# Residual adds, gate copies and normed tiles moved on VectorE's queue, and one weight tile on the queue of the DMAs, in a fused trunk layer

## What is computed

```python
def rms_norm(x, g):
    y = x * lax.rsqrt(jnp.mean(x * x, axis=-1, keepdims=True) + EPS)
    return y * g

def swiglu(x, wg, wu, wd):
    return (jax.nn.silu(x @ wg) * (x @ wu)) @ wd

def trunk_layer(x, ...):
    x = x + 0.5 * swiglu(rms_norm(x, g_ffn1), w_ffn1_gate, w_ffn1_up, w_ffn1_down)
    y, st = hybrid_mixer(rms_norm(x, g_mix), ..., w_in, b_gates, ..., w_out)
    x = x + y
    x = x + 0.5 * swiglu(rms_norm(x, g_ffn2), w_ffn2_gate, w_ffn2_up, w_ffn2_down)
    return x, st
# hybrid_mixer: p = rms_norm(x) @ w_in, cut into q, k, v, o (4 heads of an mLSTM),
# q, k, v, g (4 heads of a retention) and 8 gate rows; both scanned in chunks of 64
# tokens with carried states; the heads' normed outputs times w_out.
# At the end y = rms_norm(x, g_final), token by token, and the new states.
```

## Time and profile before

| | before |
|---|---|
| median of 3 runs | 1066.2 us (1065.99 to 1066.45) |
| profiled execution, its time | 1065.86 us |
| its span | 1064.1 us |
| TensorE, matmuls | 1040.7 us busy (98%), 8229 |
| TensorE, weight loads | 1030.3 us (97%), 8229 |
| VectorE | 792.1 us (74%), 1497 instructions |
| ScalarE | 515.3 us (48%), 943 |
| POOL | 215.1 us (20%), 190 |
| DMA | 142.14 MB, mean 134 GB/s |

### The profile page before, as it was taken

The page is one execution under the profiler, slowest core; times in us unless marked ns, Lnnn a source line. Parts: engine busy times, 40 slices in busy tenths (PEclk is TensorE's granted clock), DMA queues, the critical chain, the costliest instruction groups (busy, mean ns, idle before and its releaser), DMA issues.

```text
span 1064.1 us, 20973 instructions
## 1 busy us (share of the span) xinstructions
PE 1040.7 (98%) x8229; PEld 1030.3 (97%) x8229; DVE 792.1 (74%) x1497; ACT 515.3 (48%) x943; POOL 215.1 (20%) x190
## 2 busy tenths in 40 slices
PE   9999999999999979999999999999999999999996
PEld 8999999999999979999999999999999999999996
DVE  6985688987889866556655556588458889789986
ACT  6453366645665635333322223445336664466654
POOL 1100212222221211211332222210012222222120
PEclk9999999999999989999999999999999999999999
DMA  7536988789887566345354324543778888888852
GB/s 224 127 79 143 199 169 174 155 182 183 166 169 154 87 136 137 68 75 76 75 78 70 72 63 77 140 90 70 188 158 166 169 173 170 177 170 170 167 102 95
DMA packets 271963, 142.14 MB, mean 134 GB/s; under 512 B 10348, under 2 KB 269588, under 8 KB 271736
## 3 DMA queue, kind: packets, MB, share of 16 engines
q1 hardware_dynamic: 215736, 110.99, 42.2%
q0 software_dynamic: 56048, 29.79, 21.9%
q10 hardware_dynamic: 80, 0.02, 0.0%
HBM read 135.80 MB, written 3.29 MB: 131 GB/s over the span
## 4 chain that ended last, share of the span: by engine, by line
PE 82%; DVE 9%; issue 4%; DMA 2%; ACT 2%; SPq 0%; DVEq 0%; ACTq 0%
PE dense L857 35%; PE dense L733 34%; PE core_banks L857 4%; PE core_banks L733 3%; DVE w_lo L1732 3%; DVE h_raw L1762 1%; PE dense L803 1%; DMA w_raw<-in_w_in 1%; ACT w_hi L1269 1%; PE core_banks L1069 1%; PE core_banks L1084 1%; DVE h_op L1774 1%; DVE xT L1861 1%; PE core_banks L1087 1%; PE core_banks L1059 1%
## 5 line engine op out<-in xcount | busy, mean ns | idle before, releaser
L1269 ACT ACTIVATE w_hi<-w_src 128x512 fp32r<-128x512 f32 x182 | 113.2, 628 | 98.2 <-PE dense L857 55.8
L1269 ACT ACTIVATE w_hi<-w_raw 128x512 fp32r<-128x512 f32 x182 | 112.9, 629 | 82.7 <-PE dense L857 60.2
L857 PE MATMUL dense<-h_op,w_hi 128*128 128x272 f32 x768 | 147.9, 291 | 1.9 <-DVE xT L1861 1.7
L1732 DVE TENSOR_TENSOR w_lo<-w_raw,w_hi 128x512 fp32r<-128x512 f32 x182 | 123.8, 687 | 33.2 <-ACT w_hi L1269 31.6
L1732 DVE TENSOR_TENSOR w_lo<-w_src,w_hi 128x512 fp32r<-128x512 f32 x182 | 124.6, 688 | 29.8 <-ACT w_hi L1269 27.7
L733 PE MATMUL dense<-xg_hi,w_hi 128*128 128x272 f32 x672 | 142.3, 293 | 0.4 <-DVE rows L2197 0.4
L733 PE MATMUL dense<-xg_lo,w_hi 128*128 128x272 f32 x672 | 138.9, 288 | 0.0
L733 PE MATMUL dense<-xg_hi,w_lo 128*128 128x272 f32 x672 | 138.8, 287 | 0.0
L857 PE MATMUL dense<-x_late_hi,w_hi 128*128 128x272 f32 x432 | 125.8, 291 | 4.4 <-DVE rstd L1807 3.6
L857 PEld LDWEIGHTS dense<-h_op,w_hi 128*128 128x128 f32 x768 | 120.2, 188 | 4.6 <-DVE xT L1861 4.5
L857 PE MATMUL dense<-x_op_hi,w_lo 128*128 128x272 f32 x432 | 124.5, 288 | 0.0
(11 more groups left out here) (363 smaller groups left out, 2386.7 us busy)
## 6 DMA issues: line engine op xcount, KB each, us to landing
w_raw<-in_w_ffn_up SPq DMA_DIRECT2D x91, 256.0 KB, 4.2
w_src<-in_w_ffn_gate SPq DMA_DIRECT2D x90, 256.0 KB, 4.5
w_raw<-in_w_in SPq DMA_DIRECT2D x32, 512.0 KB, 9.2
w_src<-in_w_ffn_down SPq DMA_DIRECT2D x40, 256.0 KB, 4.3
w_raw<-in_w_ffn_down SPq DMA_DIRECT2D x40, 256.0 KB, 3.2
w_src<-in_w_ffn_gate POOLq DMA_DIRECT2D x36, 256.0 KB, 5.5
w_raw<-in_w_ffn_up POOLq DMA_DIRECT2D x36, 256.0 KB, 5.9
w_raw<-in_w_ffn_down SPq DMA_DIRECT2D x16, 384.0 KB, 6.1
```

Source lines behind the costliest of these rows:

```text
L857: last = nc.tensor.matmul(out, w[:, k, :], x, start=o in OPENS and k == 0 and m == 0, stop=k == KH - 1 and m == 2, skip_group_check=o not ...
L1269: nc.scalar.activation(block_of(w_hi, n, o), source(e, o), ACT.Copy).then_inc(block_hi, 1)
L1732: nc.vector.tensor_tensor(block_of(w_lo, n, o), source(g % 2, o), block_of(w_hi, n, o).bitcast(F32), ALU.subtract)\
```

## The change

Six moves; nothing is computed differently.

1. In a pair step, the h work (`sum_h`, `h_to_lo`) of a block product stands behind the copy out of the bank, where it stood ahead of it.
2. In an up step the two `split_lo` of `w_down` tiles stand one block product later (o = 4 and 6 in place of 3 and 5).
3. In the first down step of a chunk the adds to the residual stand further ahead, and the weight sum `sum_t2` behind the add of product 2.
4. At the mixer's start, the first w_in tile's rounding (ScalarE) and its low part (VectorE) stand behind the last two normed tiles and their squares; two of the sums of squares stand ahead of it, too.
5. SP issues the third w_in tile ahead of the last down step's blocks, in place of behind the first two tiles. Its wait for a slot is that of every plain tile.
6. At the end: the last pair's first two turns stand one block product later; one `last` turn goes into the last product ahead of its last tile of the sum; one chunk's scaling and one of VectorE's copies stand further ahead; in the last step of the second half two of the sums of squares stand two ranks earlier.

```diff
@@ load (SP) @@
-                if U_IN <= s < U_IN + RAW - 1:
-                    sp.wait_ge(block_lo, BLOCKS * STEP_LAST + (2, BLOCKS, 6, 6)[s % RAW])
+                if s in (U_IN, U_IN + 1, U_IN + 3):
+                    sp.wait_ge(block_lo, BLOCKS * STEP_LAST + (2, BLOCKS, 6)[s % RAW])
                 elif s >= RAW:
                     sp.wait_ge(w_lo_ready, s - RAW + 1 + step * i)
@@ ffn (SP) @@
                     for d in range(DOWNS):
+                        if step_of_down(n, c, d) == STEP_LAST:
+                            load_in(0, 2)
                         load_blocks(n, step_of_down(n, c, d), down_quarter(w_down, c, d))
...
+            def load_in(h, u):
+                col = (h // H) * 4 * H * P + u * H * P + (h % H) * P
+                load(0, U_IN + 4 * h + u, 0, w_rows(w_in)[:, :, col:col + P], DT)
...
-                    load(0, U_IN + 4 * h + u, 0, in_v[:, :, col:col + P], DT)
+                    if h or u != 2:
+                        load_in(h, u)
@@ down_pair (TensorE) @@
-                    turns = {1: 2 * d - 2, 2: 2 * d - 1} if d == DOWNS - 1 else {3: 2 * d - 2, 5: 2 * d - 1}
+                    turns = {2: 2 * d - 2, 3: 2 * d - 1} if d == DOWNS - 1 else {3: 2 * d - 2, 5: 2 * d - 1}
...
-                    part(o, range(KH)).then_inc(product_done, 1)
+                    if o == 6 and g == 2 * STEPS - 1:
+                        part(o, range(last_k))
+                        turn_last(1)
+                        part(o, range(last_k, KH)).then_inc(product_done, 1)
+                    else:
+                        part(o, range(KH)).then_inc(product_done, 1)
                 if g == 2 * STEPS - 1:
-                    turn_last(1)
                     turn_last(2)
@@ down_pair (ScalarE) @@
                     split_hi(0, U_GATE, 0)
-                    split_hi(0, U_IN, 0)
                     for j in (DT - 1, DT - 2):
                         x_ready(n, j)
                         normed_hi(0, j, None, G_MIX, 0)
                         square_end(n, j)
+                    split_hi(0, U_IN, 0)
@@ last_part (ScalarE) @@
                 scale_chunk(0, ACT_COLS)
+                scale_chunk(1, ACT_COLS)
                 last_times_gain(DT - 2, 1, 6)
-                scale_chunk(1, ACT_COLS)
@@ next_lo (VectorE) @@
-                elif g % STEPS == STEP_DOWN and o in (3, 5):
-                    split_lo(0, U_DOWN[n] + (o - 3) // 2, 0)
+                elif g % STEPS == STEP_DOWN and o in (4, 6):
+                    split_lo(0, U_DOWN[n] + (o - 4) // 2, 0)
@@ pair (VectorE): these lines go from ahead of the copies of o = 3, 4, 5 to behind them @@
                     if deferred:
                         for h_o in ((), (1,), (2,), (4, 5), (), (), ())[o] if e == 0 else ():
                             sum_h(n, k, h_o)
                         for h_o in (((), (), (), (), (0,), (1,), (3,)), ((2,), (4,), (5,), (6,), (), (), ()))[e][o]:
                             h_to_lo(n, k, h_o)
@@ down_pair (VectorE), d == 0 @@
                     h_to_lo(n, k, 3)
+                    take_down(n, c, d, 0)
                     h_to_lo(n, k, 2)
-                    take_down(n, c, d, 0)
+                    take_down(n, c, d, 1)
                     h_to_lo(n, k, 4)
-                    take_down(n, c, d, 1)
                     take_down(n, c, d, 3)
                     h_to_lo(n, k, 5)
                     next_lo(n, g - 1, 6)
-                    sum_t2(g + 1)
                     take_down(n, c, d, 2)
                     h_to_lo(n, k, 6)
+                    sum_t2(g + 1)
@@ down_pair (VectorE), d > 0 @@
+                    if g % STEPS == STEP_LAST and rank in ((1, 2) if n else (3, 4)):
+                        add_end(n, DT - 4 + (rank in (2, 4)))
...
-                    if g % STEPS == STEP_LAST and rank in (3, 4):
-                        add_end(n, DT - 4 + (rank == 4))
...
-                        if o == 5:
-                            split_lo(0, U_IN, 0)
-                            normed_lo(0, DT - 1, 1, G_MIX, 0)
-                            add_end(n, DT - 1)
...
                             scale_last(0, DVE_COLS)
+                            scale_last(1, DVE_COLS)
+                            take_last(1)
                 if g == STEP_LAST:
+                    normed_lo(0, DT - 1, 1, G_MIX, 0)
                     normed_lo(0, DT - 2, 1, G_MIX, 0)
+                    add_end(n, DT - 1)
                     add_end(n, DT - 2)
+                    split_lo(0, U_IN, 0)
                 if g == 2 * STEPS - 1:
...
-                    scale_last(1, DVE_COLS)
-                    take_last(1)
```

More of the change, by code:

```diff
@@ L671, in ffn @@
                     for d in range(DOWNS):
+                        if step_of_down(n, c, d) == STEP_LAST:
+                            load_in(0, 2)
                         load_blocks(n, step_of_down(n, c, d), down_quarter(w_down, c, d))
+            def load_in(h, u):
+                col = (h // H) * 4 * H * P + u * H * P + (h % H) * P
+                load(0, U_IN + 4 * h + u, 0, w_rows(w_in)[:, :, col:col + P], DT)
             ffn(0, w_ffn1_gate, w_ffn1_up, w_ffn1_down)
-            in_v = w_rows(w_in)
             for h in range(2 * H):
                 for u in range(4):
-                    col = (h // H) * 4 * H * P + u * H * P + (h % H) * P
-                    load(0, U_IN + 4 * h + u, 0, in_v[:, :, col:col + P], DT)
+                    if h or u != 2:
+                        load_in(h, u)
                 if h == 0:
@@ L1898, in pair @@
                         sum_t4(g + 1)
-                    if deferred:
-                        for h_o in ((), (1,), (2,), (4, 5), (), (), ())[o] if e == 0 else ():
-                            sum_h(n, k, h_o)
-                        for h_o in (((), (), (), (), (0,), (1,), (3,)), ((2,), (4,), (5,), (6,), (), (), ()))[e][o]:
-                            h_to_lo(n, k, h_o)
                     if o == 3:
@@ L1920, in pair @@
                             up_third_gated(p, Q)
+                    if deferred:
+                        for h_o in ((), (1,), (2,), (4, 5), (), (), ())[o] if e == 0 else ():
+                            sum_h(n, k, h_o)
+                        for h_o in (((), (), (), (), (0,), (1,), (3,)), ((2,), (4,), (5,), (6,), (), (), ()))[e][o]:
+                            h_to_lo(n, k, h_o)
                     if not (ends and o == 6):
```

## The result

The changed kernel took 1068.55 us (median of 9 runs, 1066.33 to 1070.79), the kernel before 1066.11 us (9 runs, 1065.86 to 1067.71) beside it: a ratio of 1.002, 95% interval 1.0011 to 1.0029. The forecast was 1059.2 us. The profiled execution of after is the slowest of its nine, 1070.79 us with a span of 1069.1 us, so the losses read from it are some 2 us larger in all than the median's.

The account below looks back on a forecast made before the run. TensorE's own work was taken to set the time, with some 13 us of waits to win in a 1064.1 us span. Gains 4.2 + 1.3 + 0 + 0.7 + 0.8 = 7.0 us gave 1059.2 us against the 1066.2 us median; range 1055.5 to 1063.8.

Parts of the forecast that it names:

- Pair steps: Gate steps' last block product: the copy out of the bank ends 0.35 us sooner, twelve times; 4.2 us gained (0 to 5.5).
- First down steps: First down step of each chunk: adds free the bank sooner; 0.33 us four times, 1.3 us gained.
- Second half step's down: Second FFN, w_down split behind up_second: the 0.8 us wait goes, but TensorE waits longer for the last SiLU; 0 gained (0 to 0.8).
- Mixer's order: Mixer's start: second w_in product 2.4 us sooner, less 1.7 us for the clock; 0.7 us gained (-1.0 to 2.4).
- The price of the clock: Mixer's start: 0 to 6.8 us at half clock behind 5.2 us of idle time costs half; middle taken, 1.7 us.
- (c): Rival, mixer's start: the clock holds through the moved idle time; 1057.5 us, chance 0.05.
- End: Kernel's end: a turn one product later, a square sum moved, less three turns in the last product; 0.8 us gained (-0.5 to 1.7).
- The third w_in tile: Last down step: issued early on SP, hidden by 5.8 us spare before VectorE reads the accumulated block; cost taken as 0.
- (d): Rival, last down step: early w_in tile holds up the blocks; slower, 1068.3 us if landing at 357.7; chance 0.12.
- the third of the prediction's signs of being wrong: Ahead of the last down step: the prediction is wrong if VectorE waits for a DMA there.
- (a): Rival, mixer: first two w_in tiles come sooner than 12.4 and 15.8 us, 6.8 us gained there; 1053.1 us, chance 0.08.
- (b): Rival, pair steps: they keep their wait since something other than gate_second ends it; 4.2 us missing, 1063.4 us, chance 0.12.

Follow-up runs that it names:

- e1: The kernel put back: the changed kernel, with SP issuing the third w_in tile behind the first two again, as before; 1058.3 us, ratio 0.9928.
- e10: The kernel before plus pair-step copies ahead of h work, w_down low parts one product later, and the new first-down-step order; 1059.52 us, ratio 0.994.
- e4: The kernel before with only the mixer's new order: last two normed tiles and their squares ahead of the first w_in tile; 1065.45 us, ratio 0.9992.
- e5: e1 with the fourth w_in tile issued in the third one's place, behind the second, nothing fetched early; 1066.94 us, one run.
- e9: e8 with POOL making the second w_in tile's low part, in place of VectorE behind the gate rows; 1057.65 us, ratio 0.9923.
- e6: e1 with the first two w_in tiles loaded early to their own memory; first rounding and root's table load ahead of last normed tiles; 1072.02 us.
- e8: e1 with the root ahead of the second w_in tile's rounding, its table load earlier, that tile's low part behind the gate-row copies; 1057.55 us.
- e11: e8 with ScalarE's table load for the exponential ahead of the third w_in tile's rounding; 1054.22 us, ratio 0.9891.
- e3: The changed kernel, with SP's queue waiting for the second w_in tile's landing before issuing the rotation table and states; 1065.44 us.

## Why the prediction failed, step by step

**Pair steps: right.** 0.35 us twelve times; all twelve gaps are 0.24 us.

**First down steps: right in the sum.** -0.61 us for the bank and +0.15 and +0.16 for two smaller gaps: 0.30, forecast 0.33. One of the two gaps is at the step's first wait, where the forecast had nothing (the four waits of 0.2 us for `h_op` in the list of after).

**Second half step's down: right in after, too low elsewhere.** In after the place gave 0.3 us: the wait of 0.8 us went, and TensorE stood 1.03 us ahead of the first down product, since ScalarE's rounding again waited for the second w_down tile. In the kernel put back and in e10 the place gained 1.4 us, above its bound of 0.8; in the former that tile had landed. The landing decides, and it differs from kernel to kernel.

**Mixer's order: right, as far as the noise lets it be seen.** 0.7 us forecast, 0.8 measured alone (e4), with the idle time moved as described; 0.5 us of wait was left ahead of the norm sums, where the prediction had none. The price of the clock, 1.7 us, was 1.9 in after and 2.6 in the kernel put back, within its bounds of 0 to 3.4. By the rule that the prediction names from the Trainium skill (TensorE: Matmul & The Clock Gate, section "HAM oscillation — how this bites in real kernels") the loss stands; the stretch at 403.63 agrees, and it is the dense one that no row of before showed. Of the rivals, (c) is out.

**End: right.** 0.65 us in all, forecast 0.8; its parts were not measured one by one.

**The third w_in tile: wrong, and it decided.** The sum took 0 for it, and it cost some 10 us (e1): 3.9 us in the last down step of after and the rest mostly at the mixer's start. Rival (d) had the first place and the sign, with a chance of 0.12, but not its working. It put the point from which the tile costs at a landing at 350.3; the tile landed at 348.77, 15.1 us after its issue, which by that reckoning costs nothing. Two readings failed. First, (d) let the block behind the tile land 1.9 us after it; it landed 4.0 us after it, at 352.75, 11.1 us from its issue. And the spare time was reckoned for one reader, VectorE's sum (358.21 in before; it started at 357.96, having waited 1.31 us for the accumulation, much as the third of the prediction's signs of being wrong has it). But POOL's queue carries the squares' DMAs behind the blocks' accumulations. These timelines are POOL's and ScalarE's of after:

```profile
353.04 1.28 POOL L2438 DMA_DIRECT2D w_raw<-in_w_ffn_down  x1 [16.09 <-DMA w_raw<-in_w_ffn_down]
355.11 1.28 POOL L2440 DMA_DIRECT2D w_raw<-in_w_ffn_down  x1 [0.79 <-DMA w_raw<-in_w_ffn_down]
355.86 1.45 POOL L2432 DMA_DIRECT2D sum_ident<-sq  x1
```

```profile
361.49 0.66 ACT L1422 ACTIVATE sq<-xT 128x544 f32<-128x544 f32 x1 [2.90 <-DMA sum_ident<-sq]
362.06 0.61 ACT L1279 ACTIVATE w_hi<-w_raw 128x512 fp32r<-128x512 f32 x1
```

The first accumulation went out at 353.04, 6.6 us later than in the earlier trace rows; the square's DMA behind it landed at 361.5; ScalarE stood 2.9 us for it, with the rounding of a block behind that, and from there VectorE's low part and its adds, and TensorE, were late. The prediction named POOL's queue, but only its accumulations. Second, the landing of the second w_in tile, 15.8 us, was carried over as a constant though the change altered what follows it on the queue. It took 23.5 us, and the root, which stands behind its rounding on ScalarE, went with it, and with the root the 11.5 us of wait:

```profile
393.87 1.06 ACT L1225 ACTIVATE w_hi<-w_raw 128x1024 fp32r<-128x1024 f32 x1 [9.36 <-DMA w_raw<-in_w_in]
394.94 1.28 ACT L1247 ACT_TABLE_LOAD   x1
396.24 0.71 ACT L1247 ACTIVATE rstd<-core_banks,eps 128x544 f32<-128x544 f32 x1
```

**Rivals (a) and (b): out.** The first two tiles took 13.5 and 23.5 us, not less, though a neighbour had been read 20 us before; and the pairs lost their wait.

Why the second w_in tile took so long with another tile behind it is open (see e5). Without that one step the forecast of 1059.2 us stands against 1058.3 measured (e1). That it comes so near is in part luck: 1.4 us of e1's gain come from the second half step's down, which the sum put at 0.

## What to carry to other kernels

A load that is moved ahead can cost what everything beside and behind it on the DMA engines waits, on all queues: before taking it at nothing, list each transfer in its time and the reader that is latest with it, the small ones too. A landing time read from a trace belongs to the order of transfers around it and is not a constant once that order is changed. Where an engine waits for a value that stands in a queue behind a transfer it doesn't need (here the root behind a weight tile), moving the transfer cost 10 us, and moving the value ahead, with the next table load, was worth 4.

## What the runs showed of the hardware

The first of the w_in tiles (512 KB) to be issued, and the early one, took 12.4 to 15.5 us in every kernel here, a block of the other weights (256 KB) 3.0 to 4.9 in the last down step of before. In these two stretches, of before and of after (columns as in the earlier trace rows), DMA engines were busy to about the same share, and moved a third as much while the early tile was under way:

```profile
340.00:350.00 10.00, 9.57 (x75) 9.14 (x74) 9.66 (x20) 5.51 (x9) 1.36 (x2) 1.00 0.61 149
```

```profile
338.00:348.00 10.00, 10.00 (x78) 9.61 (x77) 9.97 (x21) 5.25 (x9) 0.00 (x0) 1.00 0.59 48
```

Other traffic isn't needed for it. In this stretch of before only w_in tiles were under way:

```profile
369.00:380.00 11.00, 11.00 (x90) 11.00 (x89) 5.05 (x11) 1.72 (x5) 3.12 (x7) 1.00 0.52 52
```

What makes w_in slow was not settled (its rows are 16416 bytes apart, those of the other weights 11264 or 4096).

Ahead of the second w_in product TensorE kept a granted clock of 1.00 behind idle pieces of 0.5, 1.1 and 1.5 us (e9, e6, e8 and e11), and ran its next 3.4 us at 0.50 (1.2 GHz) behind 4.1 and 11.5 us (e1, after). Elsewhere the length of the piece alone didn't decide: behind the 1.7 us at line 1119 of e8 the next 4 us were granted 0.68 on the mean, and behind the 2.2 us in the last down step of after 0.63, while e3 kept 1.00 behind 1.9 us in that same step:

```profile
364.98 0.39 PE L864 MATMUL dense<-h_op,w_hi 128*128 128x272 f32 x1 [1.87 <-DVE xT L1872]
```

```profile
364.99:368.39 3.40, 3.40 (x27) 3.40 (x28) 2.58 (x6) 1.81 (x3) 0.86 (x1) 1.00 0.17 31
```

The prediction had only one such piece to go by, 3.5 us.
